# Hybrid diffusion layer on one core: a rewritten stage ahead of the input projection

## What is computed

```
m = silu(cvec) @ w_ada + b_ada             # cvec: c for latents, c_ctx for context
sh1, sc1, g1, sh2, sc2, g2 = split(m, 6)
h = rmsnorm(x) * norm_mix * (1 + sc1) + sh1
proj = h @ w_in                            # 1024 x 1024
pool_out = window means of proj[:512] minus the token, mixed by channel
ssm_out  = bidirectional diagonal scan of proj[512:], b_bar = ((a_bar - 1) / a) * b
x = x + g1 * (concat(pool_out, ssm_out) @ w_out)
x = x + g2 * (square(relu(h2 @ w_mlp1)) @ w_mlp2)      # h2 from sh2, sc2
```

## Time and profile before

| | |
|---|---|
| median of 3 runs | 1416.01 us (1414.13 to 1416.47) |
| span of the profiled execution | 1413.4 us |
| span minus median | -2.6 us |
| busy in the span | PE 1267.7, DVE 907.1, POOL 598.0, ACT 306.2 us |
| first matmul of the input projection | 89.72 us |

### The profile page before, as it was taken

One profiled execution on the slowest core, in us unless ns is written; L12 is line 12 of the kernel. 1 busy time (PEld: TensorE's weight loads), 2 busy tenths in 40 slices (PEclk: granted clock), 3 DMA queues, 4 the chain that ended last, 5 costly groups with the idle time before them and its releaser, 6 DMA issues.

```text
span 1413.4 us, 19045 instructions
## 1 busy us (share of the span) xinstructions
PE 1267.7 (90%) x6399; PEld 1065.7 (75%) x6399; DVE 907.1 (64%) x1463; ACT 306.2 (22%) x595; POOL 598.0 (42%) x458
## 2 busy tenths in 40 slices
PE   4879997885558899799999999999999999999995
PEld 0269894152258786599899889989988998998893
DVE  1787788988873675884564565466456546645648
ACT  3462333020212310651011111101111110111113
POOL 1100313941002559525633743563474356347436
PEclk9979998888769999999999999999999999999998
DMA  8711366527124610020110110111011011101003
GB/s 216 246 30 31 112 141 116 184 99 133 46 94 107 188 30 32 29 76 29 60 55 20 43 59 30 30 59 52 22 45 59 30 30 59 51 23 45 30 0 134
DMA packets 82835, 101.64 MB, mean 72 GB/s; under 512 B 31974, under 2 KB 66442, under 8 KB 82412
## 3 DMA queue, kind: packets, MB, share of 16 engines
q1 hardware_dynamic: 62360, 85.59, 20.5%
q0 software_dynamic: 3136, 12.06, 3.2%
q10 hardware_dynamic: 17300, 3.48, 1.3%
HBM read 89.53 MB, written 9.49 MB: 70 GB/s over the span
## 4 chain that ended last, share of the span: by engine, by line
PE 67%; DVE 15%; POOL 6%; issue 3%; ACT 3%; DMA 2%; SPq 2%; ACTq 1%; DVEq 0%; POOLq 0%
PE bank L1105 20%; PE bank L1107 20%; PE bank L1106 20%; POOL acc L458 4%; POOL acc L468 2%; DVE step_r L951 2%; DVE states L954 2%; DVE step_q L947 2%; DVE step_q L948 2%; PE bank L1118 1%; DMA raw<-in_w_ada 1%; SPq L349 1%; PE bank L1149 1%; DVE step_p L946 1%; ACT h_tile L505 1%
## 5 line engine op out<-in xcount | busy, mean ns | idle before, releaser
L468 POOL TENSOR_TENSOR acc<-acc,gated 128x512 f32<-128x512 f32 x288 | 401.3, 1393 | 392.2 <-DVE gated L1069 353.2
L1105 PE MATMUL bank<-x_hi,w_hi 128*128 128x384 f32 x992 | 332.6, 335 | 0.1
L1106 PE MATMUL bank<-x_lo,w_hi 128*128 128x384 f32 x992 | 332.0, 335 | 0.0
L1107 PE MATMUL bank<-x_hi,w_lo 128*128 128x384 f32 x992 | 332.0, 335 | 0.0
L1069 DVE TENSOR_TENSOR gated<-bank,gate_b 128x512 f32<-128x512 f32 x288 | 194.4, 688 | 117.6 <-PE bank L1107 104.0
L1105 PE MATMUL bank<-w_hi,f_hi 128*128 128x512 f32 x576 | 224.4, 390 | 1.4 <-DVE w_lo L1050 0.8
L1107 PE MATMUL bank<-w_hi,f_lo 128*128 128x512 f32 x576 | 224.4, 390 | 0.0
L1106 PE MATMUL bank<-w_lo,f_hi 128*128 128x512 f32 x576 | 224.3, 389 | 0.0
L1059 DVE TENSOR_TENSOR f_tmp<-relu 128x384 f32<-128x384 f32 x96 | 65.0, 677 | 211.6 <-ACT relu L715 211.3
L715 ACT ACTIVATE relu<-bank 128x384 f32<-128x384 f32 x96 | 47.2, 493 | 648.9 <-PE bank L1107 647.3
L1105 PEld LDWEIGHTS bank<-x_hi,w_hi 128*128 128x128 f32 x992 | 186.7, 188 | 1.1 <-issue 0.5
(11 more groups left out here) (239 smaller groups left out, 1481.3 us busy)
## 6 DMA issues: line engine op xcount, KB each, us to landing
raw<-in_w_mlp SPq DMA_DIRECT2D x64, 512.0 KB, 3.5
raw<-in_w_ada SPq DMA_DIRECT2D x48, 512.0 KB, 5.0
x_tile<-in_x_sample POOLq DMA_DIRECT2D x8, 512.0 KB, 8.0
raw<-in_w_in SPq DMA_DIRECT2D x8, 512.0 KB, 4.1
raw<-in_w_out SPq DMA_DIRECT2D x8, 512.0 KB, 6.9
acc<-in_x_sample SPq DMA_DIRECT2D x1, 4096.0 KB, 13.5
out<-acc SPq DMA_DIRECT2D x8, 512.0 KB, 2.6
inv_count_b<-in_inv_count POOLq DMA_DIRECT2D x4, 576.0 KB, 4.5
```

Source lines behind the costliest of these rows:

```text
L468: GP.tensor_tensor(a, a, BT[i % 4][:], ALU.add).then_inc(s.acc, 1)
L1105: mm(out, sh_, mh, start=first, stop=False)
L1106: mm(out, sh_, ml, start=False, stop=False)
L1107: return mm(out, sl, mh, start=False, stop=last)
```

## The change

- The three transfers of b bring rows as they lie in memory, 64 rows of 4 KB (`BR`), and PE turns them with 32 transposes into banks 0 to 3, which ACT copies out.
- `b_ada` is loaded as 48 rows beside the other vectors and turned with them; the bias rows, their matmuls and the row transposes go.
- A block of w_ada is now the stationary operand, in 8 pieces of 128 x 128, with the 2 columns of `silu(c)` moving (`ada_cols`), so shift and scale arrive as columns. The same is done for parts 3 and 4 later; the gates stay rows.
- POOL issues all token tiles at once, and behind them the first two blocks of `w_in` (`WIN`), which leave the SP ring.
- Tile k is turned right behind block 8 + k on PE, without scale and shift. DVE and ACT copy the turned tile into a buffer `XT` for all tokens. DVE does its tiles ahead of the powers and of `b_bar`.
- Scale and shift are then applied by channel block, on 384 (256 and 128) tokens at once, in place; rounding and remainder go by half a group of 4 x 384.
- The projection takes group 0 of blocks 0 and 1 first, then group 1 of both, group 2 of both, then block by block as before. It begins a group when half the channels are ready.

```diff
-        for t in range(TT):
-            if t:
-                gp.wait_ge(s.ada_used, t)
...
+        for w in range(2):
+            gp.dma_start(WIN[w][:].rearrange("p (k f) -> p k f", k=KB), in_v[:, :, w * P:(w + 1) * P]).then_inc(s.win_in, 16)
...
-        for dst, top, bot in ((BX, ssm_b_re, ssm_b_im), (BY, ssm_b_im, ssm_b_re)):
-            act.dma_start(dst[0:N], top[0].rearrange("d g n p -> n (d g) p")).then_inc(s.b_in, 16)
-            act.dma_start(dst[N:P], bot[0].rearrange("d g n p -> n (d g) p")).then_inc(s.b_in, 16)
+        for k, v in enumerate((ssm_b_re, ssm_b_im, ssm_b_re)):
+            act.dma_start(BR[:, k, :], v[0].rearrange("d g n p -> (d g) (n p)")).then_inc(s.br_in, 16)
...
+        for k, (dst, done) in enumerate(((BX, s.b_re_out), (BY, s.b_im_out))):
+            act.wait_ge(s.b_turn, k + 1)
+            for hf in range(2):
+                S.activation(dst[:, :, 8 * hf:8 * hf + 8].rearrange("n q p -> n p q"),
+                             BANK[2 * k + hf][:].rearrange("n (p q) -> n p q", q=Q), ACT.Copy).then_inc(done, 1)
...
+        def affine0(g):
+            for k in range(4, KB):
+                for cond, lo, hi in cond_cols(g):
+                    S.activation(XT[:, k, lo:hi], XT[:, k, lo:hi], ACT.Identity,
+                                 scale=ADA[0][:, cond, k:k + 1], bias=ADA[1][:, cond, k:k + 1]).then_inc(s.h0_aff_a, 1)
...
+        for t in range(TT + 2):
+            if t < TT:
+                act.wait_ge(x_in[t], 16 if t < L else 16 * L)
+                stats(t, XS[t][:], SQ0[:], 0)
+            if t >= 2:
+                evict(t - 2)
+        for w in range(2):
+            split_in(w)
+        act.wait_ge(s.ada0, 2)
+        for g in range(NG):
+            affine0(g)
...
+                round_hi0(g, hf)
...
+        for t in range(TT + 1):
+            if t < TT:
+                normed(t, XS[t][:], XS[t][:], 0)
+            if t:
+                evict(t - 1)
...
+        for w in range(2):
+            split_in(w)
+        dve.wait_ge(s.ada_used, N_ADA0)
...
+        affine0(0)
+        for g in range(NG):
+            if g + 1 < NG:
+                affine0(g + 1)
+            for hf in range(2):
+                round_lo0(g, hf)
...
+            for c in range(KB):
+                last = mm(out[:, 2 * c:2 * c + 2], RAW[n % 4][:, c * P:(c + 1) * P], cv, start=(first and k == 0 and c == 0), stop=(k == KB - 1),
+                          skip_group_check=True)
...
+        for k in range(KB):
+            ada_cols(KB + k, BANK[7][:, 112:128], k, False)
+            turn_tile(k, XS[k], 0)
+        turn_tile(TT - 1, XS[TT - 1], 0)
```

More of the change, by code:

```diff
@@ L196, in build, with cond_cols, b_cols, in_raw @@
     PARTS = [1, 0, 2, 3, 4, 5]
+    B_ROW = 36
+    IN_ORDER = [(0, 0), (1, 0), (0, 1), (1, 1), (0, 2), (1, 2)] + [(mb, g) for mb in range(2, KB) for g in range(NG)]
+    IN_DONE = [5, 6] + [3 * (mb + 1) for mb in range(2, KB)]
+    AFF0 = [4, 8, 16]
+    def cond_cols(g):
+        return [(0, g * TG, (g + 1) * TG)] if g < 2 else [(0, 2 * TG, LAT), (1, LAT, T)]
+    def b_cols(part):
+        return COL[:, B_ROW + KB * part:B_ROW + KB * (part + 1)]
+    def in_raw(w):
+        return WIN[w][:] if w < 2 else RAW[(FIRST_IN + w - 2) % 4][:]
     def raw_landed(eng, n):
@@ L504, in affine @@
             for k in range(4, KB):
[L505 to L511, removed]
+                S.activation(HT1[t % 2][:, k, :], turn_banks(t, 6)[1][:, (k - 4) * P:(k - 3) * P], ACT.Identity,
+                             scale=ADA[2][:, cond, k:k + 1], bias=ADA[3][:, cond, k:k + 1]).then_inc(s.aff_a, 1)
@@ L645, in _ @@
              .then_inc(s.kk_ready, 1)
-        for k in range(6, 8):
-            ada_row(k)
+        gate_row(2, 6)
+        gate_row(3, 7)
         for gi in range(4):
@@ L976, in _ @@
         tt(fin, fin, qs, ALU.add).then_inc(s.cx_h, 1)
-        dve.wait_ge(s.acts, 4 + 64 + 4)
-        for cond in range(2):
-            then(stt(ADA[2][:, cond, :], ADA[2][:, cond, :], 1.0, COL[:, 24:32], ALU.add, ALU.mult))
+        dve.wait_ge(s.acts, 4 + 64 + 2)
+        ada_part(ADA[3], ADA[3][:], 3)
+        ada_part(ADA[2], ADA[2][:], 4)
+        ada_scale(ADA[2], 24)
         for w in range(2):
@@ L1107, in three @@
             return mm(out, sl, mh, start=False, stop=last)
-        pe.wait_ge(s.vec_in, 80)
+        pe.wait_ge(s.vec_in, 96)
         pe.wait_ge(s.id_ready, 1)
-        PE.transpose(BANK[7][:, 0:36], VEC[:], ID[0:36, 0:36]).then_inc(s.pe_small, 1)
-        def ada_unit(n, banks, k):
+        PE.transpose(BANK[7][:, 0:84], VEC[:], ID[0:84, 0:84]).then_inc(s.pe_small, 1)
+        pe.wait_ge(s.br_in, 48)
+        br = BR[:].rearrange("q r (n p) -> q (r n) p", p=SP)
+        for k in range(2):
+            for p in range(SP):
+                last = PE.transpose(BANK[2 * k + p // 8][:, p % 8 * Q:p % 8 * Q + Q], br[:, k * N:k * N + P, p], ID[0:Q, 0:Q])
+            last.then_inc(s.b_turn, 1)
@@ L1115, in ada_unit, with ada_cols @@
+        def ada_cols(n, out, k, first):
             raw_landed(pe, n)
             cv = COL[:, 0:16].rearrange("p (a k) -> p a k", a=2)[:, :, k]
-            for hf in range(2):
-                last = mm(BANK[banks[hf]][0:2, :], cv, RAW[n % 4][:, hf * 512:hf * 512 + 512], start=(k == 0), stop=False)
+            for c in range(KB):
+                last = mm(out[:, 2 * c:2 * c + 2], RAW[n % 4][:, c * P:(c + 1) * P], cv, start=(first and k == 0 and c == 0), stop=(k == KB - 1),
+                          skip_group_check=True)
@@ L1136, in _ @@
[L1136 to L1140 removed]
         def turn_tile(t, src, base):
             pe.wait_ge(s.xn, base + t + 1)
[L1145 to L1147 removed]
+            if base == 0:
+                if t == 1:
+                    pe.wait_ge(s.b_im_out, 2)
+                if t >= 2:
+                    pe.wait_ge(s.xt_a, t - 1)
+                    pe.wait_ge(s.xt_d, t - 1)
+            elif t >= 2:
+                pe.wait_ge(s.aff_d, 4 * (t - 1))
+                pe.wait_ge(s.aff_a, 4 * (t - 1))
@@ L1150, in turn_tile @@
             last.then_inc(s.tr, 1)
-        for t in range(TT):
-            turn_tile(t, XS[t], 0)
+        pe.wait_ge(s.silu_done, 1)
+        for k in range(KB):
+            ada_cols(k, BANK[7][:, 96:112], k, True)
+        pe.wait_ge(s.ada_used, KB)
+        pe.wait_ge(s.tabs, 3)
+        for i in range(4):
+            last = PE.transpose(BANK[6][:, i * Q:(i + 1) * Q], TAB[:, i, :], ID[0:Q, 0:Q])
+        last.then_inc(s.pe_small, 1)
+        for k in range(KB):
+            ada_cols(KB + k, BANK[7][:, 112:128], k, False)
+            turn_tile(k, XS[k], 0)
+        turn_tile(TT - 1, XS[TT - 1], 0)
         a = 0
```

360 lines of the change are left out of this document (167 added, 193 removed).

## The result

| | before | after |
|---|---|---|
| median | 1416.2 us | **1440.7 us** (1440.1 to 1442.1, 4 runs) |
| ratio | | 1.018, 95% interval 1.0162 to 1.0191 |
| span of the profiled execution | 1413.4 us | 1439.0 us |
| last token tile turned | 90.1 us | 90.0 us |
| first matmul of the projection | 89.72 us | 115.04 us |

The change makes the kernel 24.5 us slower; the forecast was 1400.4 us, and the time lies above its range, 1395 to 1418. The two first matmuls are 25.3 us apart, the two spans 25.6: the whole loss stands ahead of the projection.

The account below looks back on a forecast made before the run. It took a chain PE projection, DRAM transfers, DVE scan, PE as the bound; first projection matmul 72.9 instead of 89.72 gains 16.8 us, less 1.2 cold start: 1413.4 - 15.6 = 1397.8, plus 2.6 to the median: 1400.4 us, range 1395 to 1418.

Parts of the forecast that it names:

- end of the last tile at 48.0 us: Before the projection: last w_ada block lands at 45.3 us, then PE needs 2.7 us for its product and two tiles.
- Price of a block: On PE, a w_ada block of 16 load-and-matmul pairs costs 1.95 us at the low clock, 1.0 at the high one.
- without 14 columns in two passes: Pair price: 0.145 us measured with 16 columns, less 0.023 us for columns not streamed, gives 0.122 at the low clock.
- rival 2: PE before the projection: low clock and dearer block, 2.3 us (1420 us) or 3.1 us (1433 us); chance 13%.
- The clock: PE runs at the high clock in the second half of the w_ada blocks, where blocks and token tiles alternate.
- 1.8 us for both is under the 2.8 us in which a block arrives.: Second half of w_ada: PE's block plus eight transposes, 1.0 and 0.8 us, fit within a block's arrival time.
- the far bound: Transfers: last w_ada block lands at 50 us instead of 45.3, at the 314 GB/s of 40 to 60 us.
- The tail: Last tile to first projection matmul: from 48.0 to 72.9 us, including 15.7 for powers and b_bar without cover.
- The rest follows: Behind the projection: DVE about 2.0 us later against PE, covered by 3.53 us idle at the scan; nothing lost.
- the cold start of the projection: PE starts the projection at the low clock after standing still for 25 us; 1.2 us lost, between 0 and 1.9.
- the first sign of being wrong: The forecast is wrong if PE's clock stands at 0.50 while w_ada blocks and token tiles alternate.
- Rival 1: PE before the projection stays at the low clock, last tile at 61.6 us, net gain 2.0, 1414.0 us; chance 16%.

Follow-up runs that it names:

- e9: The changed kernel with the later column blocks (parts 3 and 4, under the scan) written to banks 0 and 1, following the gate's dense products without a pause; 1441.5 us.
- e1: The changed kernel with its first 16 w_ada blocks multiplied in row form again, rows copied out by ACT and turned by 16 small transposes; 1419.0 us, ratio 1.0031.
- e5: The changed kernel, column form kept, with b turned behind block 3 of w_ada instead of ahead of block 0; 1439.3 us, ratio 1.018.
- e6: e1 (row form) with b turned behind block 3 of w_ada instead of ahead of block 0; 1415.8 us, ratio 1.0009 to the kernel before.
- e11: e6 with POOL issuing token tile t only once t blocks of w_ada are used; 1409.2 us, ratio 0.996 to the kernel before.
- e3: e1 with DVE's powers behind tile 0's eviction and b_bar in two halves behind tiles 2 and 4; 1412.5 us, ratio 0.999 to the kernel before.
- e7: e6 with tables turned behind block 3, powers right behind them, b_bar's six steps behind separate tiles, last tile's copy behind first scale and shift; 1400.3 us, ratio 0.9909.
- e4: The changed kernel with two dense 512-column products, results thrown away, behind each of part 3's 8 column blocks under the scan; 1445.9 us.

## Why the prediction was wrong, by its own steps

**The step that failed is PE's: end of the last tile at 48.0 us, measured 90.0.** It was a chain of three choices.

1. *Price of a block.* By "without 14 columns in two passes" I brought a pair down from 0.145 to 0.122 us at the low clock and to half of it at the high one. Measured 0.214 and 0.11. The row of 16 columns in the earlier trace rows stands in a pattern with other shapes, and its distance of 0.29 us for two pairs did not hold for a run of full loads of 128 x 128. It was the distance of passes, not of loads. The loads of the same place, in PEld's timeline of the kernel before, had the right price:

```profile
394.63 0.55 PEld L1289 LDWEIGHTS bank<-states,from_state 128*128 128x128 f32 x2
395.06 0.55 PEld L1286 LDWEIGHTS bank<-u_chunks,local 128*128 128x128 f32 x2
```

Two loads in 395.06 - 394.63 = 0.43 us are 0.215 each, at a granted clock of 0.50. The earlier trace rows was near too, 1.56 / 8 = 0.195 for a full load, which I used only as the far end of rival 2. The same length had me price a tile's eight transposes at 1.56 and 0.8 us; they took 1.74 (51.21 to 52.95) and 1.02.

2. *The clock.* I took the high clock in the second half because PE would have no gaps. e9 shows that full occupancy does not hold it: the clock fell in a stretch with PE busy 2.00 of 2.00 us., transposes at 1.00, was no counterexample for the column form. e1 confirms what I read from it for transposes, 1.00 over 24 us of tiles among row blocks; but there dense row products stood between. The Trainium skill, TensorE: Matmul & The Clock Gate, Part 4, has the full clock not engage for transposes; e1's window disagrees for a mixture with dense work. In the kernel after the clock was low before any token tile was turned: the 128 pairs from 19.64 to 47.1 us hold no transpose, and in e5 the first 64 pairs, 13.79 us, follow nothing but one small transpose. So the columns alone keep it low from the start, and e9, with no transposes in the stretch, shows that they also let it fall.
3. *"1.8 us for both is under the 2.8 us in which a block arrives."* From it I let the transfers set the end. At 2.4 GHz a block costs 1.8 us in either form and a tile 1.02, together 2.83 in e1, e6 and e11: as much as the 2.8 in which I had a block arrive. PE was then the bound in e1 and e6, and level with the transfers in e11. The arrival was too early as well: in e11 PE still waited for block 14 until 52.23 us, and I had block 15 landed at 45.3, at 50 by the far bound. This step would have failed without the column form too: e6's last tile came at 63.5, e11's at 59.8.

**Split of the 42 us.** From the kernel after to e1, the form: 22.7. e1 to e6, PE and ring held up by b: 3.8. e6 to e11, all tiles requested at once: 3.7. There remain 11.8, from 59.8 to 48.0. Counted back from 45.3 at 2.8 us a block, the forecast had block 8 at 25.7; e11 began it at 33.76, behind a wait for it. So 8.1 of the 11.8 us stand ahead of block 8: the first block lands at 12.5 us, and from 4 to 20 us the transfers move 266 GB/s where I had 371. Seven blocks at 3.04 us instead of 2.8 are 1.7, and 4.7 us instead of 2.7 from the last block on are 2.0. Why the transfers are that slow at first was not tried. The order of undoing matters (in the column form the middle two were 1.3 and 2.6 us), so the parts are sizes, not laws.

**Right.** The tail: 24.9 us from last tile to first matmul, measured 25.0; powers and `b_bar` from 90.61 to 106.2, 15.6 for 15.7, bare as said. PE's pause ahead of the projection is 25.1 us in all six kernels that left this part alone. In it ACT's scale and shift was dearer, 2.50 us for four where I had 1.8. silu came at 7.28 for "near 6" (the earlier trace rows had ACT held until 17.72), and b's rows took 2.9% of the transfer engines over 100 us where the earlier trace rows has 11.5%. But I had them landed at about 10 us, and PE waited for them until 15.89:

```profile
q10 hardware_dynamic: 480, 0.82, 2.9%
```

*The rest follows:* "Rest" in the table is 1321.9 to 1326.4 us for every kernel, with first matmuls 42 us apart. DVE came to the scan 28.2 us later (238.29 for 210.07) for 25.3 of the first matmul, a lag of 2.9 where I had 2.0. The idle time of 3.53 us in the earlier trace rows took up most of it and is down to 1.29, and the third pass starts 26.0 us later:

```profile
239.69 1.34 DVE L977 TENSOR_TENSOR pair_p<-states,pow_re 128x1136 f32<-128x1136 f32 x1 [1.29 <-ACT ctx_final L638]
```

The later column blocks under the scan cost nothing, as said: the "rest" is the same, though they ended 36 us later than the old ones (335.04 for 299.1), 10 us more than the shift of the first matmul.

*One term came out small by no merit of its reasoning:* the cold start of the projection, priced at 1.2 us, cost 0.1 here (3.0 us at the low clock for 2.9 before). In e1, behind the same pause, it was 5.9 us.

**The rivals.** Rival 2, low clock and a dearer block, is what happened, with a block of 3.4 us beyond its dearest price of 3.1, which gave 1433 us and lay above the range. It had 13%, because I made rivals 1 and 2 depend on a clock that I thought unlikely to stay low; the first sign of being wrong that I named, 0.50 while tiles and blocks alternate, is the one that came. Rival 1's price of a block was wrong as well. The same page of the Trainium skill, section LDWEIGHTS, gives 107 ns for 128 columns; e9 agrees at 2.4 GHz (0.11 us a pair) and the kernel after does not at 1.2 (0.214). I had applied it to the low clock and got 1410. With the measured block of 3.43 us in place of 1.95, rival 1's own sum gives 15.8 + 8 x 3.43 + 0.6 + 8 x (3.43 + 1.56) + 1.6 = 85.4 us for the last tile; the 3.8 us by which b came later bring it to 89.2, measured 90.0.

## What to carry to other kernels

- Swapping the operands of a thin product trades streamed columns for weight loads. At equal clock that cost the same here (3.50 and 3.51 us), but the engine fell to 1.2 GHz under it and its neighbours, the transposes, paid too. A busy share of 100% is no proof of the high clock: where no row shows this form of instruction at 1.00, forecast it at 0.50. Read its price from the loads' own timeline.
- When two kinds of work are laced into one engine, add them and compare with the arrival rate at both clocks before saying which one is hidden.
- Work taken out of its cover needs a new place in pieces as small as the gaps. With three lumps among the tiles PE stood 5.11 and 0.78 us for DVE (e3); with powers ahead of the tiles and one step of `b_bar` per tile it stood for none (e7). The projection began 10.2 us earlier in e7, but b's place and the copy of the last tile were changed with it, so that is no price of the lumps alone.

## What the runs showed of the hardware

- A run of 128 x 128 fp32 loads with 2 columns streamed let the granted clock fall from 1.00 to 0.50 with PE busy all the time (e9, seen once). From a cold start it never rose under them: 27.5 us of such pairs alone and 43 more with tiles between in the kernel after, 13.8 us alone in e5.
- A pair of load and 2-column pass took 0.11 us at 1.00 and 0.214 at 0.50: it scales with the clock.
- Alternating such a block with as much dense work did not raise the clock from 0.50 in 56 us (e4), while row blocks of 1.81 us with eight transposes of 1.02 held 1.00 (e1).
- A longer run of transposes is not proved harmless. The 32 transposes of b stand in one piece from 24.28 to 27.94 us in e6, with PE busy 2.00 of 2.00 us, and the clock fell behind them; in e11 the same piece, 21.55 to 25.21, was followed by 1.00. What the fall cost in e6 is not known: PE waited 1.23 us for block 8 soon after. The windows of e6:

```profile
26.00:28.00 2.00, 2.00 (x20) 1.93 (x19) 0.00 (x0) 1.72 (x2) 0.00 (x0) 1.00 1.06 295
28.00:30.00 2.00, 2.00 (x4) 0.28 (x4) 0.00 (x0) 2.00 (x4) 0.00 (x0) 0.53 1.05 260
```

- The time at the low clock at the projection's start does not follow the length of the pause ahead of it: behind the same 25.1 us it was 3.0 us in the kernel after and 5.9 in e1, and 5.3 behind the 8.6 us of e7. Before the change, with no pause there but a clock already low, it was 2.9.
